# Layer 0's set-up and modulation: two phases, or one

## The reference, cut to what matters

```python
mod = silu(cond) @ mod_w[layer] + mod_b[layer]   # 3072 values: shift, scale, gate
h = x * (1 + scale) + shift                      # modulated input of the layer's projection
# ... layer branches on h ...
# x = layer_norm(ALPHA * x + gate * branch_output)
```

## Time and profile before

| | us |
|---|---|
| Median of 3 runs | 3125.31 |
| Lowest, highest | 3123.38, 3126.24 |
| Profiled execution, its own time | 3122.36 |
| Its span (first to last instruction) | 3120.5 |
| TensorE busy | 2566.5 (82%) |
| VectorE busy | 1594.2 (51%) |
| ScalarE busy | 900.2 (29%) |
| GpSimd busy | 740.2 (24%) |

### The profile page before, as it was taken

The page is one execution under the profiler, slowest core; times in us unless marked ns, Lnnn a source line. Parts: engine busy times, 40 slices in busy tenths (PEclk is TensorE's granted clock), DMA queues, the critical chain, the costliest instruction groups (busy, mean ns, idle before and its releaser), DMA issues. The chain is left out here.

```text
span 3120.5 us, 54817 instructions
## 1 busy us (share of the span) xinstructions
PE 2566.5 (82%) x23550; PEld 2181.4 (70%) x23550; DVE 1594.2 (51%) x2413; ACT 900.2 (29%) x1458; POOL 740.2 (24%) x739
## 2 busy tenths in 40 slices
PE   4799999974788864476785999999599999998787
PEld 1577777764677753366563877777499999998665
DVE  2127888542445614776265655556535545464233
ACT  0113333311132222564212323232233333332211
POOL 0211111116556641111222111111012221111422
PEclk7899999986889966587887999999799999999898
DMA  6612544542233413111452233332412222210621
GB/s 260 214 57 80 179 123 153 175 143 76 76 76 113 115 30 90 44 49 36 153 115 72 88 112 108 112 98 100 169 48 75 89 75 89 75 55 1 219 93 59
DMA packets 290447, 319.51 MB, mean 102 GB/s; under 512 B 109727, under 2 KB 235110, under 8 KB 287646
## 3 DMA queue, kind: packets, MB, share of 16 engines
q1 hardware_dynamic: 289136, 312.64, 31.7%
q10 hardware_dynamic: 1070, 3.37, 0.3%
HBM read 203.32 MB, written 112.56 MB: 101 GB/s over the span
## 5 line engine op out<-in xcount | busy, mean ns | idle before, releaser
L2814 PE MATMUL PS<-Q,K 128*128 128x128 f32 x2560 | 296.6, 278 | 31.2 <-DMA K<-k_d 24.1
L2814 PEld LDWEIGHTS PS<-Q,K 128*128 128x128 f32 x2560 | 293.1, 194 | 33.8 <-issue 28.1
L2935 POOL TENSOR_TENSOR weights_lo<-weights,weights_hi 128x1664 fp32r<-128x1664 f32 x32 | 121.4, 3793 | 566.4 <-ACT weights_hi L2893 566.4
L2841 PE MATMUL PS<-V_hi,weights_hi 128*128 128x258 f32 x832 | 239.1, 287 | 5.3 <-DVE H L3044 2.7
L379 PE MATMUL PS<-hT_hi,w_in_hi 128*128 128x512 f32 (+1 forms) x640 | 239.7, 375 | 0.0
L380 PE MATMUL PS<-hT_lo,w_in_hi 128*128 128x512 f32 (+1 forms) x640 | 236.4, 369 | 0.0
L381 PE MATMUL PS<-hT_hi,w_in_lo 128*128 128x512 f32 (+1 forms) x640 | 236.1, 369 | 0.0
L2842 PE MATMUL PS<-V_lo,weights_hi 128*128 128x258 f32 x832 | 236.0, 284 | 0.0
L2843 PE MATMUL PS<-V_hi,weights_lo 128*128 128x258 f32 x832 | 235.2, 283 | 0.0
L379 PE MATMUL PS<-h_hi,w_in_hi 128*128 128x512 f32 (+1 forms) x624 | 227.3, 364 | 5.1 <-PEq L112 5.1
L2315 PE MATMUL PS<-w_out_hi,y_in_hi 128*128 128x512 f32 x416 | 168.9, 406 | 70.7 <-DVE y_in_lo L2253 39.1
(11 more groups left out here) (406 smaller groups left out, 5661.6 us busy)
## 6 DMA issues: line engine op xcount, KB each, us to landing
chunk_in<-in_d SPq DMA_DIRECT2D x40, 512.0 KB, 3.4
w_in<-in_e_w_in_dram SPq DMA_DIRECT2D x30, 512.0 KB, 5.0
xnew<-in_o_w_in_dram SPq DMA_DIRECT2D x30, 512.0 KB, 6.1
in_d<-xnat SPq DMA_DIRECT2D x20, 640.0 KB, 5.9
modw<-in_mod_w_dram SPq DMA_DIRECT2D x8, 1536.0 KB, 19.1
xnat<-in_mod_w_dram SPq DMA_DIRECT2D x8, 1536.0 KB, 7.4
v_d<-xnew SPq DMA_DIRECT2D x16, 640.0 KB, 3.0
k_d<-xc SPq DMA_DIRECT2D x16, 640.0 KB, 2.9
```

The costliest lines, as they stand in the source:

```text
L2814: last = pe.matmul(PS[:, 4 + x % 4, (j - j0) * P:(j - j0 + 1) * P], K[:, kt, j * P:(j + 1) * P], Q[:, kt, i * P:(i + 1) * P], start=(kt == ...
L2841: pe.matmul(out, wh, VH[:, j, q], start=(j == seen[0]), stop=False)
L2935: pool.tensor_tensor(WL[n % 2][:], W[:, n % 2], WH[n % 2][:].bitcast(F32), ALU.subtract).then_inc(s["w_lo"], 1)
```

## The change

`setup_phase` and layer 0's use of `modulate_split` are replaced by one phase, `front_phase` with `front_program`. `project_phase` calls it, with the buffers of the first weight tile and of the lr weights allocated before it.

- Weights come in a ring of four buffers of 1 MB. Loads 0 to 7 hold the shift and scale columns (2048) of the eight tiles, loads 8 to 11 the gate columns (1024) of two tiles each. From the fifth on a load waits until TensorE is done with the load four before. The order on SyncE's queue: constants, loads 0 to 7, context and latent input, loads 8 to 11, first value weights, lr weights, then the column stores and the two gate stores.
- TensorE multiplies loads 0 to 7, turns the row, waits for columns and input, and runs the 24 jobs in banks 4 to 7. The parameter rows are transposed after job 3; the gate products of loads 8 to 11 follow jobs 6, 8, 11 and 13; the six gate pieces follow jobs 17 to 22.
- VectorE adds the bias for shift and scale in two instructions, evicts the jobs, copies the parameter columns after job 5, and after job 15 waits for the last gate product and adds the gate's bias in two instructions.
- ScalarE copies the gate pieces, between its roundings. The gates are stored as two transfers of 512 KB.
- The split of the first value tile moves into `values_phase`: ScalarE's part is its first instruction there, GpSimd's its first too, and the third value tile's load now waits for both.
- The one phase has 31 semaphores, where the two had 24 and 9.

```diff
-def setup_phase(nc, A, G, xnat):
+def front_phase(nc, A, G, xnat, hi, lo, w, wlr, win):
...
+    gate, ring = [gates_sb[:, i] for i in range(2)], [modw[:, i] for i in range(4)]
+    LOADS = KT + KT // 2
+    jobs = [(k, at, n) for k in range(KT) for at, n in ((0, CTX), (CTX, 512), (CTX + 512, 512))]
+    GATES_AT = {6: 0, 8: 1, 11: 2, 13: 3}
+    ROWS_AT, PIECES_AT, COLS_AT = 15, 17, 3
...
+            def load(i):
+                if i >= 4:
+                    sp.wait_ge(s["mod_k"], i - 3)
+                if i < KT:
+                    sp.dma_start(ring[i % 4], A.mod_w[0, i * P:(i + 1) * P, 0:2 * D]).then_inc(ring_in[i % 4], 16)
+                else:
+                    k = 2 * (i - KT)
+                    sp.dma_start(ring[i % 4].rearrange("p (k n) -> p k n", k=2),
+                                 A.mod_w[0, k * P:(k + 2) * P, 2 * D:].rearrange("(k p) n -> p k n", p=P)).then_inc(ring_in[i % 4], 16)
...
+            for i in range(KT):
+                load(i)
+            sp.dma_start(xnat[:, 0:CTXCH, :], A.ctx[0].rearrange("(c p) d -> p c d", p=P)).then_inc(s["x_in"], 16)
+            sp.dma_start(xnat[:, CTXCH:NCH, :], A.x[0].rearrange("(c p) d -> p c d", p=P)).then_inc(s["x_in"], 16)
+            for i in range(KT, LOADS):
+                load(i)
+            sp.dma_start(w[:, 0], win[:, :, GV:GV + P]).then_inc(s["w_in"], 16)
+            sp.dma_start(wlr[:], win[:, :, GLR:GLR + 32]).then_inc(s["small_in"], 16)
+            sp.wait_ge(s["cols_sb"], 3)
...
+            for g in range(2):
+                sp.wait_ge(s["gate_sb"], 3 * (g + 1))
+                sp.dma_start(A.gates_d[g], gate[g]).then_inc(s["stored"], 16)
+            sp.wait_ge(s["stored"], 5 * 16)
...
+            def shift_scale(k):
+                pe.wait_ge(ring_in[k % 4], 16 * (k // 4 + 1))
+                for off, n, groups in ((0, 512, (0, 1, 2)), (512, 256, (0, 1))):
+                    for g in groups:
+                        last = pe.matmul(PS[group_rows(g), off // 512, 0:n], G.cond[:, k, :], ring[k % 4][:, g * GCOLS + off:g * GCOLS + off + n],
+                                         start=(k == 0), stop=(k == KT - 1))
...
+            def gates(i):
+
+                x = KT + i
+                pe.wait_ge(ring_in[x % 4], 16 * (x // 4 + 1))
+                for j in range(2):
+                    k = 2 * i + j
+                    for g, off, n, _ in GATE_PIECES:
+                        at = j * D + g * GCOLS + off - 2 * D
+                        last = pe.matmul(PS[group_rows(g), 2 + off // 512, 0:n], G.cond[:, k, :], ring[x % 4][:, at:at + n],
+                                         start=(k == 0), stop=(k == KT - 1))
...
+            for k in range(KT):
+                shift_scale(k)
+            pe.wait_ge(s["mod_row"], 1)
+            mod_turn(pe, G, 4, modrow).then_inc(s["vec_ps"], 1)
+            pe.wait_ge(s["vec_sb"], 1)
+            pe.wait_ge(s["x_in"], 32)
+            for n, (k, at, m) in enumerate(jobs):
+                if n >= 4:
+                    pe.wait_ge(s["taken"], n - 3)
+                for i in range(m // P):
+                    last = pe.transpose(PS[:, 4 + n % 4, i * P:(i + 1) * P], xnat[:, at // P + i, k * P:(k + 1) * P], G.c("ident"))
+                last.then_inc(s["turned"], 1)
+                if n == COLS_AT:
+                    pe.wait_ge(s["rows_in"], 16 * n_rows)
...
+                if n in GATES_AT:
+                    gates(GATES_AT[n])
+                if PIECES_AT <= n < PIECES_AT + 6:
+                    j = n - PIECES_AT
+                    if j == 0:
+                        pe.wait_ge(s["gate_row"], 2)
+                        pe.wait_ge(s["cols_sb"], 3)
+                    if j >= 2:
+                        pe.wait_ge(s["gate_sb"], j - 1)
+                    gate_matmul(pe, G, PS[:, j % 2, :], modrow, j // 3, j % 3).then_inc(s["gate_ps"], 1)
...
+                act.activation(hi[:, k, at:at + m], full[:, n % 4, 0:m], ACT.Copy).then_inc(s["hi_ok"], 1)
+                if PIECES_AT <= n < PIECES_AT + 6:
...
+                    act.wait_ge(s["gate_ps"], j + 1)
+                    act.activation(gate[j // 3][:, to:to + size], PS[:, j % 2, 0:size], ACT.Copy).then_inc(s["gate_sb"], 1)
...
+                if n == ROWS_AT:
+                    dve.wait_ge(s["mod_k"], LOADS)
+                    gs = PS[:, 2:4, :].rearrange("p a b -> p (a b)")
+                    dve.tensor_tensor(modrow[64:96, 512:GCOLS], gs[64:96, 512:GCOLS], modb[64:96, 512:GCOLS], ALU.add).then_inc(s["gate_row"], 1)
+                    dve.tensor_tensor(modrow[96:128], gs[96:128, 0:GCOLS], modb[96:128], ALU.add).then_inc(s["gate_row"], 1)
...
             for q in (2, 3):
-                if q == 3:
+                if q == 2:
+                    sp.wait_ge(s["first_hi"], 1)
+                    sp.wait_ge(s["first_lo"], 1)
+                else:
...
+            act.activation(wvh[:, :, 0:P], w[:, 0], ACT.Copy).then_inc(s["first_hi"], 1)
             act.wait_ge(s["zeroed"], 1)
...
+            pool.wait_ge(s["first_hi"], 1)
+            pool.tensor_tensor(wvl[:, :, 0:P], w[:, 0], wvh[:, :, 0:P].bitcast(F32), ALU.subtract).then_inc(s["first_lo"], 1)
+            pool.wait_ge(s["first_lo"], 1)
...
-            modulate_split(nc, G, 0, xnat, hi, lo, full, first_loads, 1, first_high, first_low)
...
-                    setup_phase(nc, A, G, xnat)
```

More of the change, by code:

```diff
@@ L208, in sb @@
             return ctx.enter_context(nc.sbuf_tensor(n, s, F32))
[L209 to L231, removed]
-                for h in range(2):
[L233 to L264, removed]
-                    for h in range(2):
[L266 to L315, removed]
@@ L455, in values_phase @@
     PS = G.PS
-    sems = ("w_in0 w_in1 hi_ok lo_pool lr_ps lg_ok m_in0 m_in1 mod_k zeroed modb_in mod_row vec_ps vec_sb gate_ps gate_sb "
+    sems = ("w_in0 w_in1 first_hi first_lo hi_ok lo_pool lr_ps lg_ok m_in0 m_in1 mod_k zeroed modb_in mod_row vec_ps vec_sb gate_ps gate_sb "
             "v_ps v_sb v_out0 v_out1 small step")
@@ L509, in _ @@
             mod(0)
+            pe.wait_ge(s["first_hi"], 1)
+            pe.wait_ge(s["first_lo"], 1)
             pe.wait_ge(s["hi_ok"], 3)
@@ L584, in project_phase @@
         w = sb("w_in0", [P, 2, KT, P])
+        wlr = sb("w_lr", [P, KT, 32])
+        front_phase(nc, A, G, xnat, hi, lo, w, wlr, win)
         wh = [sb(f"w_in0_hi{i}", [P, KT, P], F32R) for i in range(2)]
@@ L587, in project_phase @@
         outs = sb("p_out", [P, OUTS0, T])
-        with nc.sbuf_tensor("w_v_hi", [P, KT, 4 * P], F32R) as wvh, nc.sbuf_tensor("w_v_lo", [P, KT, 4 * P], F32R) as wvl, \
-                nc.sbuf_tensor("w_lr", [P, KT, 32], F32) as wlr:
-            def first_loads(sp, sem, small):
-                sp.dma_start(w[:, 0], win[:, :, GV:GV + P]).then_inc(sem, 16)
-                sp.dma_start(wlr[:], win[:, :, GLR:GLR + 32]).then_inc(small, 16)
-                return 1
-            def first_high(act):
-                return act.activation(wvh[:, :, 0:P], w[:, 0], ACT.Copy)
-            def first_low(pool):
-                return pool.tensor_tensor(wvl[:, :, 0:P], w[:, 0], wvh[:, :, 0:P].bitcast(F32), ALU.subtract)
-            full = outs[:].rearrange("p i t -> p (i t)")[:, 0:4 * 512].rearrange("p (i t) -> p i t", i=4)
-            modulate_split(nc, G, 0, xnat, hi, lo, full, first_loads, 1, first_high, first_low)
+        with nc.sbuf_tensor("w_v_hi", [P, KT, 4 * P], F32R) as wvh, nc.sbuf_tensor("w_v_lo", [P, KT, 4 * P], F32R) as wvl:
             values_phase(nc, A, G, hi, lo, free, win, w, wh, wl, wvh, wvl, wlr)
```

100 lines of the change are left out of this document (added).

## The result

| | us | against before |
|---|---|---|
| Before, median of 4 runs in the same session | 3125.77 | |
| Changed, median of 4 runs (3102.74 to 3109.51) | 3108.14 | ratio 0.9937, 95% interval 0.9921 to 0.9952 |
| Before, second session, 18 runs | 3125.68 | |
| Changed, second session, 6 runs | 3112.76 | 0.9954, 0.9939 to 0.9969 |
| Before, third session, 11 runs | 3129.63 | |

The change is faster. Between the medians of a session it gains 17.6, 12.9 and 16.3 us, by the recorded ratios 14 to 20 us; 16.5 were forecast.

A forecast was written before the change was run, and what follows sets the result against it. The prediction took a start chain of three stages, each ending before the next begins, as the bound. Values stage 16.7 us earlier less 0.2 gives 16.5 us; against the median 3125.31 that is 3108.8 us, range 3101 to 3118.

The forecast's parts named there:

- Step 1: Input load: behind the shift and scale columns it lands at 38.8 us, turns start at 38.9; ring waits cost nothing.
- Step 2: TensorE in the turns: four gate tiles at 3.0 us, last 24 transposes 2.5 us, through at 58.1 us.
- Step 3: Gate row: VectorE needs 3.9 us after the last gate product, to 62.0; TensorE waits about 2 us.
- Step 4: Gate pieces and 20 transposes: low clock taken, 6.9 + 3.9 = 10.8 us, to 72.8; high 3.5 + 2.1.
- Step 5: Phase end: last gate store lands at 75.6, 31 semaphores take 2.7 us, values stage at 78.3, 16.7 us earlier.
- Step 6: Values stage: the first weight tile's split moved into it costs 0.2 us, bounds 0 and 2.5.

The follow-up runs named there:

- a1: Changed kernel with the input loaded behind the four gate tiles instead of ahead of them; values stage at 91.27 us, total 3125.49 us (one run).
- b2: b1 with the transposes of the parameter rows behind the eighth tile instead of the third; 3112.97 us, 0.9962 of before.
- b1: Kernel before with the input loaded behind the eighth weight tile instead of the sixth; 3124.62 us, 0.9998 of before.
- v1: Changed kernel with the six gate pieces and their store moved from the turns into the values stage; 3106.87 us, 0.9939 of before.
- a2: Changed kernel with seven of eight k steps of the gate products cut to 16 columns (gates wrong); values stage at 76.91 us, total 3108.63 us (one run).
- a3: Changed kernel with three unread 512-column products ahead of TensorE's wait for the gate row; values stage at 77.60 us, total 3116.06 us (one run).
- v2: v1 with gate products at jobs 5, 9, 13 and 17 and VectorE's bias adds behind its last job; 3104.92 us, 0.9921 of before.
- a4: Changed kernel with 20 more, unused semaphores in the phase; values stage at 82.40 us, total 3120.70 us (one run).

## Why the prediction was right, point by point

- Step 1 held to 0.4 us: the turns started at 39.30 (38.9), the branch beside it was through at 30.5 with the columns. TensorE's wait at 39.30 is for the input, and in a1 it moved with the input's place. The ring's waits cost nothing: SyncE waited for products, but the DMA share was 1.01 to 1.04 from 4 to 48 us, so the transfers had no hole.
- Step 2 held to 0.2 us, 57.9 against 58.1, but two of its terms were off against each other. A gate tile took 2.77 us, not 3.0; the 24 transposes between the tiles took 3.3 us, not 2.5. The moment of the rise is luck too: 3.6, 4.7 and 5.7 us behind the first turn in the three profiles, and TensorE was through at 57.9, 58.4 and 58.7.
- Step 3 held: the adds ended at 62.22 (62.0), TensorE idled 2.65 us (2).
- Step 4 named the low clock rightly, but its size was off. Expected was TensorE through at 72.8; it was 75.5. From 62.28 on pieces and turns took 13.2 us, where the sum had 10.8, and both terms share the miss. Counted from start to start the pieces took 8.0 us instead of 6.9 and the 20 transposes 5.2 instead of 3.9. The 6.9 were the price of six pieces in a row at the low clock, which b2 has at 5.79 us; each piece between turns costs more than in a row (0.69 + 1.97 + 1.22 + 1.22 + 2.07 + 1.22 = 8.4 us as the trace times them, five of six at the low clock). At the high clock the prediction's 3.5 us for six in a row was right where three banks serve them in turn (b1, 3.46); v1, with five banks, has 2.85. The pieces of b1 and of b2:

```profile
51.74 3.46 PE L193 MATMUL PS<-modrow,cst 2*128 2x256 f32 x12
```

```profile
44.47 5.79 PE L193 MATMUL PS<-modrow,cst 2*128 2x256 f32 x12
```

- Step 5 had the wrong last wait, by little. The gate store was through near 77.6, but GpSimd's last low part, which the prediction took as covered, ended at 78.34 and held the phase 0.7 us longer, in all three profiles. The end of the phase then took 2.3 us, 2.7 expected. The values stage started at 80.68, 2.4 us later than forecast; the last piece was in SBUF at 75.08 instead of 72.6, which is step 4's miss, and the small errors of this step nearly cancel.
- Step 6: no cost of the moved split (GpSimd idle 4.31 us ahead of its last pair). The stage gained 1.1 us instead of losing 0.2: its first product came 16.8 us in, not 17.9, since TensorE's clock was high 3.2 us into the lr products, where before it took over 5. That did not repeat: in the second and third profile it took 4.2 and 5.3 us, and the first product came 17.4 and 17.9 us in. So 15.4 us at the first product, against 16.5 forecast, is a miss of 2.4 less a gift of 1.3, and most of the gift was chance: the other two profiles have 14.9 and 14.6.
- The total of 16.5 lies inside what the three sessions give (12.9 to 17.6 us between the medians). The agreement with 3108.8 to 0.7 us is luck: medians of the same kernel lie 5 us apart between sessions.

On the clock, TensorE had done nothing but transposes since 39.30 when it rose near 42.9, ahead of the first gate product at 43.99. In a2, where the gate products are nearly gone, it rose near 42.4 and stayed at 1.00 until 56, with TensorE busy 2.90 of 4 us from 44 to 48. The Trainium skill (TensorE: Matmul & The Clock Gate, Part 4: PE-mode transpose) says that transposes do not count as work for the full clock; by it there would have been no rise before the gate products, and these traces go on disagreeing with it.

Where the low level came from is shown in part. Behind the wait of 2.65 us it fell with the pieces (63.4) and, in v1, without them (64.3), so the pieces aren't needed for it. Without the wait it fell later (a3, 68.2), with TensorE busy throughout. What brings it down there, pieces or turns, stays open.

## What to carry to other kernels

Ask of each large load when its data is first used, and look for what lands early and waits: 24 us of waiting input were worth 9 us with two conditions moved. When work of one engine is slipped between the steps of another, its pieces must be shorter than the slack that has built up since the last one: four tiles of 2.8 us nearly fitted at every fourth job and cost 4 us at every second or third (3.8 by a2, 3.6 by v2 with the adds moved too). Judge such a change by marks in the trace close to it; behind it the same code moved the end by several microseconds either way.

## What the runs showed of the hardware

- Small loads on ScalarE's queue, all issued by 31.4 us, had landed by 35.9 in one order of the big loads and by 40.5 in another (b1, b2). What delays them was not tried.
- Clearing a semaphore at a phase's end costs 0.084 us (a4, 20 more of them). By that the 31 of this phase would take 2.6 us; the trace leaves 2.3 for the whole end, so they are nearly all of it.
- Six two-row products in a row took 2.85 us (v1) and 3.46 (b1) at the high clock and 5.79 at the low one (b2); between turns they took 8.4, mostly at the low one.
